# A chunked state space layer on three engines: inputs spread between two turns, three banks for the state products, a row broadcast moved behind the loop

## The reference

```python
def s5_mixer(x, lam_re, lam_im, log_dt, b_re, b_im, c_re, c_im, d_skip, w_glu, w_out):
    u = x.astype(f32).reshape(bsz, seq, N_GROUPS_2, SSM_GROUP)     # 64 groups of 16 channels
    ...
    bu_re = jnp.einsum('bsgc,gpc->bsgp', u, bb_re)                 # 64 complex states a group
    bu_im = jnp.einsum('bsgc,gpc->bsgp', u, bb_im)
    ...
    _, _, h_re, h_im = lax.associative_scan(_complex_linear_combine, (a_re_t, a_im_t, bu_re, bu_im), axis=1)
    y = (jnp.einsum('bsgp,gcp->bsgc', h_re, c_re) - jnp.einsum('bsgp,gcp->bsgc', h_im, c_im))
    y = y + d_skip.reshape(N_GROUPS_2, SSM_GROUP) * u
    y = jax.nn.gelu(y.reshape(bsz, seq, D_MODEL)).astype(x.dtype)
    val, gate = jnp.split(y @ w_glu, 2, axis=-1)
    return (val * jax.nn.sigmoid(gate)) @ w_out
```

## Time and profile before

| | before |
|---|---|
| median of three runs | 1990.58 us (1989.95 to 1991.3) |
| profiled execution | 1992.84 us |
| its span, first to last instruction | 1991.1 us |
| mean granted TensorE clock | 0.906 |
| TensorE busy | 1655.8 us (83%) |
| VectorE busy | 539.9 us (27%) |
| ScalarE busy | 211.1 us (11%) |
| GpSimd busy | 76.0 us (4%) |
| DMA queues, mean | 271 GB/s |

### The profile page before, as it was taken

One profiled execution on the slowest core, in us unless ns is written; L12 is line 12 of the kernel. 1 busy time (PEld: TensorE's weight loads), 2 busy tenths in 40 slices (PEclk: granted clock), 3 DMA queues, 4 the chain that ended last, 5 costly groups with the idle time before them and its releaser, 6 DMA issues. The chain is left out here.

```text
span 1991.1 us, 29124 instructions
## 1 busy us (share of the span) xinstructions
PE 1655.8 (83%) x13147; PEld 1114.5 (56%) x13147; DVE 539.9 (27%) x1285; ACT 211.1 (11%) x484; POOL 76.0 (4%) x96
## 2 busy tenths in 40 slices
PE   7999768889976999856546556689999999999998
PEld 5655435567544885534324333577786446578743
DVE  5752233432333314214211011630210022421002
ACT  2311011000100001100100000110110003211000
POOL 2000000000000100000000000320000000000000
PEclk9989889887998999978778787899999999799999
DMA  9356999998899745999999999534434334134410
GB/s 335 135 204 274 379 422 420 419 421 354 339 421 373 272 197 239 382 420 418 419 416 415 413 414 391 222 128 169 159 137 169 115 118 173 39 133 164 154 57 21
DMA packets 104442, 540.11 MB, mean 271 GB/s; under 512 B 7326, under 2 KB 9438, under 8 KB 86908
## 3 DMA queue, kind: packets, MB, share of 16 engines
q1 hardware_dynamic: 102428, 531.24, 67.0%
q0 software_dynamic: 1888, 6.95, 1.0%
HBM read 531.89 MB, written 6.29 MB: 270 GB/s over the span
## 5 line engine op out<-in xcount | busy, mean ns | idle before, releaser
L712 PE MATMUL ps<-ring,work 128*32 128x256 f32 x3968 | 285.3, 451 | 223.6 <-DMA ring<-in_moe_w_up 223.1
L712 PEld LDWEIGHTS ps<-ring,work 128*32 128x32 f32 x3968 | 158.5, 129 | 342.3 <-issue 295.6
L663 PE MATMUL ps<-hT,ring 128*128 128x256 f32 (+2 forms) x1488 | 329.5, 384 | 2.6 <-DMA ring<-in_lru_w_in 2.6
L689 PE MATMUL ps<-ring,work 128*128 128x512 f32 x768 | 331.0, 592 | 0.0
L663 PEld LDWEIGHTS ps<-hT,ring 128*128 128x128 f32 x1488 | 282.9, 191 | 47.9 <-issue 5.9
L689 PEld LDWEIGHTS ps<-ring,work 128*128 128x128 f32 x768 | 145.7, 190 | 182.2 <-issue 181.3
L724 PE MATMUL ps<-ring,multi 128*32 128x256 f32 x1984 | 127.1, 399 | 16.5 <-ACT multi L1391 12.1
L1956 DVE TENSOR_TENSOR rowb<-rowb,ps 128x128 f32<-128x128 f32 x64 | 18.4, 287 | 354.0 <-ACT rowb L1386 354.0
L1962 DVE COPY multi<-ps 128x256 f32<-128x256 f32 x64 | 27.2, 425 | 283.3 <-PE ps L724 283.3
L732 PE MATMUL ps<-rowb,hres 128*128 128x128 f32 (+1 forms) x640 | 101.9, 299 | 0.2 <-DVE rowb L1622 0.2
L724 PEld LDWEIGHTS ps<-ring,multi 128*32 128x32 f32 x1984 | 60.6, 114 | 62.9 <-ACT multi L1391 18.5
(11 more groups left out here) (434 smaller groups left out, 1363.2 us busy)
## 6 DMA issues: line engine op xcount, KB each, us to landing
ring<-in_moe_w_gate SPq DMA_DIRECT2D x62, 2048.0 KB, 18.8
ring<-in_moe_w_up SPq DMA_DIRECT2D x62, 2048.0 KB, 23.4
ring<-in_moe_w_down SPq DMA_DIRECT2D x62, 2048.0 KB, 21.1
ring<-in_w_ff SPq DMA_DIRECT2D x32, 2048.0 KB, 7.8
ring<-in_sc_w_in SPq DMA_DIRECT2D x6, 2048.0 KB, 17.9
ring<-in_lru_w_in SPq DMA_DIRECT2D x4, 2048.0 KB, 18.4
ring<-in_ssm_w_glu SPq DMA_DIRECT2D x4, 2048.0 KB, 18.7
ring<-in_lru_w_out SPq DMA_DIRECT2D x2, 2048.0 KB, 20.8
```

The costliest lines, as they stand in the source:

```text
L663: mm = pe.matmul(ps[:, bank, 0:n], w[:, k, P * c:P * c + P], hT[:, k, t0:t0 + n], start=(k == 0), stop=(k == DC - 1))
L689: mm = pe.matmul(ps[0:m, 2 + 2 * b + hf, :], left[:, kk, t0:t0 + m], w[:, k, 512 * hf:512 * hf + 512], start=(kk == 0), stop=(kk == 4 * la ...
L712: mm = pe.matmul(ps[32 * q:32 * q + 32, bank, 0:256].rearrange("p (u n) -> p u n", u=2), x[:, k, :], gu[:, k, :, P * q:P * q + P], start=( ...
```

## The change

- TensorE turns block one, waits for the statistics of the second block's norm (`ffn1_var`, 2), spreads block one, and only then turns and spreads block two. The scalar engine copies the spread inputs of block one between the turns' copies of the two blocks.
- The state products go round three banks (0, 1, 7) in place of two, wait for the rotation three groups back, and are issued a group earlier, ahead of the far product.
- Behind the near product of turn 1 TensorE issues six matmuls of `keep_busy`.
- The second half is brought back into banks 5 and 6, too, behind the first Gelu. Of the first pair of the gated projection, four of eight k-steps of both value and gate are issued behind the first Gelu alone.
- On GpSimd the broadcast of the rows of "s5" moves from ahead of the loop to behind it, and in its old place stands an addition of two columns (`pool_pair`) that nobody reads.

```diff
@@ -54,6 +54,7 @@
 SC_BANKS = ((4, 5, 2), (3, 6, 7))
 CONV_A, CONV_B = 4, 3
 SG, SC, SS = 64, 16, 64
+STATE_BANKS = (0, 1, 7)
 ST = SG * SS // P
 HEADS, NOPE, ROPE, VH = 8, 128, 64, 128
 QL, KVL = 384, 256
@@ -158,6 +159,7 @@
         marks = sb("marks", [P, MAX_ROUNDS - 1])
         first_rows = sb("first_rows", [P, 1])
         even_odd = sb("even_odd", [P, 2])
+        pool_pair = sb("pool_pair", [P, 2])
         eps_t = sb("eps_t", [P, 3])
         stats = sb("stats", [P, 3, 12])
         mean_var = sb("mean_var", [P, 3, 4])
@@ -602,7 +604,7 @@
                 pool.dma_start(tab_dram[t, :, 0:n], work[:, at_:at_ + n]).then_inc(S("tabs_stored"), 16)
             pool.wait_ge(*nth("down1", EXTRA + 1))
             broadcast_rows("ffn1")
-            broadcast_rows("s5")
+            nc.gpsimd.tensor_tensor(pool_pair[:, :], ones[:, 0:2], ones[:, 0:2], ALU.add)
             def s5_by_sine(g):
 
                 b = g % 2
@@ -623,6 +625,7 @@
                     nc.gpsimd.tensor_tensor(v[:, 1], p1[:, 1], p2[:, 0], ALU.subtract).then_inc(S("s5_v"), 1)
                 if g >= 1:
                     s5_by_sine(g - 1)
+            broadcast_rows("s5")
             broadcast_rows("mlp0")
             broadcast_rows("mla")
 
@@ -1039,7 +1042,6 @@
             rows_out("mix1", [1, 2], ["sc_out0", "sc_out1"], sc_z, NMETA, "sc_z")
             moe(1)
 
-            transposes("ffn1", [1, 2], "ffn1_normed", bank=6)
             b_map = ring[:, place["s5_tab1"], :].rearrange("p (s i n) -> p s i n", s=ST, i=2)
             w_map = ring[:, place["s5_tab2"], :].rearrange("p (s i n) -> p s i n", s=ST, i=2)
             t_map = ring[:, place["s5_tab0"], 0:2048].rearrange("p (s n) -> p s n", s=ST)
@@ -1059,13 +1061,13 @@
 
             def s5_in(g):
 
-                if g >= 2:
-                    pe.wait_ge(*nth("s5_rotated", g - 1))
+                if g >= 3:
+                    pe.wait_ge(*nth("s5_rotated", g - 2))
                 for t in range(4):
                     s = 4 * g + t
                     for i in range(2):
                         for r in halves:
-                            mm = pe.matmul(ps[r, g % 2, P * t + 64 * i:P * t + 64 * i + 64], b_map[r, s, i, :], s5_u[r, s, :],
+                            mm = pe.matmul(ps[r, STATE_BANKS[g % 3], P * t + 64 * i:P * t + 64 * i + 64], b_map[r, s, i, :], s5_u[r, s, :],
                                            start=True, stop=True)
                 mm.then_inc(S("s5_bu"), 1)
 
@@ -1095,7 +1097,9 @@
             def s5_back(h):
 
                 pe.wait_ge(*nth("s5_y", 4 * h + 4))
-                bank = (5, 0)[h]
+                if h == 1:
+                    pe.wait_ge(*nth("s5_g", 1))
+                bank = 5
                 lines = s5_yr.rearrange("p (m q) c -> p m q c", q=4)
                 for k in range(CHUNK):
                     for q in range(4):
@@ -1104,34 +1108,41 @@
                 mm.then_inc(S("s5_back"), 1)
 
             pe.wait_ge(*nth("sel_ready", 1))
-            s5_inputs(0)
-            s5_inputs(1)
+            for i in range(2):
+                transposes("ffn1", [1, 2], "ffn1_normed", only=i, bank=6)
+                if i == 0:
+                    pe.wait_ge(*nth("ffn1_var", 2))
+                s5_inputs(i)
             pe.wait_ge(*nth("s5_u_act", 2))
             pe.wait_ge(*nth("s5_u_dve", 2))
             for name in ("s5_tab0", "s5_tab1", "s5_tab2"):
                 slot_wait(pe, name)
+            s5_in(0)
             for g in range(DC + 2):
-                if g < DC:
-                    s5_in(g)
+                if g + 1 < DC:
+                    s5_in(g + 1)
                 if g >= 2:
                     s5_far(g - 2)
                 if g < DC:
                     s5_near(g)
+                if g == 1:
+                    keep_busy(6)
                 if g == 6:
                     s5_back(0)
             s5_back(1)
-            pe.wait_ge(*nth("s5_g", 2))
             for m in range(DC):
-                for i, kind in enumerate("vg"):
-                    name = f"glu_{kind}{m // 4}"
-                    if m % 4 == 0:
-                        slot_wait(pe, name)
-                    if m >= 2:
-                        pe.wait_ge(*nth("glu_done", m - 1))
-                    w = slot_view(name, DC, 512)
-                    for k in range(DC):
-                        mm = pe.matmul(ps[:, 2 * (m % 2) + i, 0:SEQ], w[:, k, P * (m % 4):P * (m % 4) + P], s5_g[:, k, :],
-                                       start=(k == 0), stop=(k == DC - 1))
+                if m >= 2:
+                    pe.wait_ge(*nth("glu_done", m - 1))
+                for k0, k1 in (((0, 4), (4, DC)) if m == 0 else ((0, DC),)):
+                    pe.wait_ge(*nth("s5_g", 1 if k1 == 4 else 2))
+                    for i, kind in enumerate("vg"):
+                        name = f"glu_{kind}{m // 4}"
+                        if m % 4 == 0:
+                            slot_wait(pe, name)
+                        w = slot_view(name, DC, 512)
+                        for k in range(k0, k1):
+                            mm = pe.matmul(ps[:, 2 * (m % 2) + i, 0:SEQ], w[:, k, P * (m % 4):P * (m % 4) + P], s5_g[:, k, :],
+                                           start=(k == 0), stop=(k == DC - 1))
                 mm.then_inc(S("glu_proj"), 1)
             rows_out("s5", [1, 2], ["s5_out0", "s5_out1"], s5_y, NMETA, "glu_done")
 
@@ -1359,6 +1370,13 @@
                     A(s5_sines[:, 0], s5_sines[:, 1], ACT.Sin, scale=2 * PI_IN).then_inc(S("rot_ready"), 1)
                     act.wait_ge(*nth("rot_ready", 2))
                     A(s5_sines[:, 1], s5_sines[:, 1], ACT.Sin, scale=-2 * PI_IN).then_inc(S("rot_ready"), 1)
+
+            def s5_inputs_out(i):
+
+                u_of = s5_u.rearrange("p (m q) c -> p q m c", q=4)
+                act.wait_ge(*nth("s5_spread", i + 1))
+                A(u_of[:, 0:2, :, 32 * i:32 * i + 32], ps[:, 4 * i:4 * i + 2, 0:SEQ].rearrange("p q (m c) -> p q m c", m=DC), ACT.Copy)\
+                    .then_inc(S("s5_u_act"), 1)
 
             def moe(l):
                 blocks = moe_blocks[l]
@@ -1423,7 +1441,11 @@
                     A(meta_acc[:, 2, :], ps[:, 5, 0:NMETA], ACT.Sqrt, scale=1.0 / D, bias=eps_t[:, 0:1]).then_inc(S("meta_sd"), 1)
                 evac_turned(f"ffn{l}", blocks[-2:], bank=6, only=0)
                 deviations(f"ffn{l}", only=1)
+                if l == 1:
+                    s5_inputs_out(0)
                 evac_turned(f"ffn{l}", blocks[-2:], bank=6, only=1)
+                if l == 1:
+                    s5_inputs_out(1)
 
             evac_turned("x", [0, 1, 2])
 
@@ -1468,11 +1490,6 @@
                 A(sc_cg[m % 2], ps[:, SC_BANKS[m % 2][0], 0:TC], ACT.Copy).then_inc(S("sc_cg_out"), 1)
             moe(1)
 
-            u_of = s5_u.rearrange("p (m q) c -> p q m c", q=4)
-            for i in range(2):
-                act.wait_ge(*nth("s5_spread", i + 1))
-                A(u_of[:, 0:2, :, 32 * i:32 * i + 32], ps[:, 4 * i:4 * i + 2, 0:SEQ].rearrange("p q (m c) -> p q m c", m=DC), ACT.Copy)\
-                    .then_inc(S("s5_u_act"), 1)
             for g in range(DC + 1):
                 if g < DC:
                     act.wait_ge(*nth("s5_summed", g + 1))
@@ -1481,7 +1498,7 @@
                     h = g // 8
                     act.wait_ge(*nth("s5_back", h + 1))
                     A(s5_g[:, 4 * h:4 * h + 4, :].rearrange("p m (c k) -> p k m c", k=CHUNK),
-                      ps[:, (5, 0)[h]:(5, 0)[h] + 2, :].rearrange("p b (k m c) -> p (b k) m c", k=2, m=4), ACT.Gelu_apprx_tanh)\
+                      ps[:, 5:7, :].rearrange("p b (k m c) -> p (b k) m c", k=2, m=4), ACT.Gelu_apprx_tanh)\
                         .then_inc(S("s5_g"), 1)
             for m in range(DC):
                 act.wait_ge(*nth("glu_proj", m + 1))
@@ -2148,7 +2165,7 @@
                 dve.wait_ge(*nth("s5_bu", g + 1))
                 if g >= 2:
                     dve.wait_ge(*nth("s5_v", g - 1))
-                bu = ps[:, b, :].rearrange("p (t i c) -> p i t c", t=4, i=2)
+                bu = ps[:, STATE_BANKS[g % 3], :].rearrange("p (t i c) -> p i t c", t=4, i=2)
 
                 def by(t):
                     return t[:, 4 * g:4 * g + 4, :].unsqueeze(1).to_broadcast([P, 2, 4, NCH])
```

## The result

| | before | changed |
|---|---|---|
| median of seven runs | 1990.58 us | 1976.32 us |
| lowest | 1985.58 us | 1966.4 us |
| ratio, 95% interval | | 0.9926 [0.9905, 0.9946] |
| profiled execution | 1992.84 us | 1980.01 us |
| its span | 1991.1 us | 1978.3 us |

Foretold were 1975.4 us, 1973.3 to 1980.6, and 0.97 for faster. One run of the first set, at 2504.6 us with a mean clock of 0.631, is left out of the ratio but stands in the median of seven; without it the median is 1973.65 us.

A forecast was written before the change was run, and what follows sets the result against it. VectorE was taken to bound the layer's three-engine ring. Gains of 1.65 + 3.05 + 5.9 + 0.6 + 4.0 = 15.2 us turn the median 1990.58 into 1975.4 us (chance 0.58), range 1973.3 to 1980.6.

The forecast's parts named there:

- What bounds the layer: State space layer's loop: VectorE is the slowest of three engines, 3.95 us a group against TensorE's 3.48; 4.0 taken.
- Rotation 2 to 7: Loop, third to last rotation: three banks and earlier state products cut 25.92 us to 20.0, gain 5.9 us (5.2 to 6.2).
- GpSimd's gap: Before the loop's first addition: a program change after the row broadcast, avoided by the new order; gain 3.05 us (2.8 to 3.5).
- The end: Behind rotation 7: 0.6 us (0 to 1.2) to the last far product, then 4.0 us (2.1 if the clock dips).
- The inputs: Ahead of the first state product: spreading block one before turning block two gains 1.65 us (1.3 to 1.8).
- It starts at 1257.6: Inputs: spreading of block one starts then, after the first block's copies (1257.56) and second block's statistics (1256.80), instead of 1260.92.
- Rival (b): Clock dips once, in the ring or at the projection, costing 1.9 or about 2 us: 1977.3 us; chance 0.15.
- Rival (a): GpSimd's gap comes from a first addition or long idling, so the early pair buys nothing: 1978.5 us; chance 0.10.
- (c): Loop: VectorE and GpSimd slow each other to 4.6 us a group, 3 us less gain: 1978.4 us; chance 0.12.
- (d): TensorE stays at half clock through the whole ring, 7.0 us a group, 12.7 us slower: 2003.3 us; chance 0.02.
- The six matmuls: Before the first far product: 2.9 us and no cost at full clock, 5.8 us at half; no gain counted alone.
- The run-to-run spread: Whole kernel: 0.7 us of spread between runs, allowed at the low side of the range.

The follow-up runs named there:

- second set: The changed kernel, unaltered, measured once more in six runs: median 1968.11 us, ratio to the kernel before 0.9907 [0.9874, 0.9939].

## Why the prediction was right, and where it was not

The forecast held, and of the five terms of its sum four held in size; the inputs came out with the wrong sign.

**What bounds the layer**: right. VectorE sets the pace at 3.94 us a group once the products come early, 3.95 was read from the earlier trace rows.

**Rotation 2 to 7** (5.9 us foretold, 6.24 measured): right, for the reason given, the order of issue. I had named the two edits of the ring together; the runs give all to one.

**GpSimd's gap** (3.05 foretold, 3.63 measured): the place and the price were right, the moment wrong. I put the change of program at the first instruction of the other kind and so had the pair added early. From a broadcast to an addition it is paid from the end of the broadcast on, and moving the rows is the whole gain: 7.25 us before, 7.16 with the rows ahead again. The pair itself stood 9.14 to 10.85 us behind its broadcast in the eleven profiles that have it, where the DMA engines are 0.99 busy with expert weights; whether that is why isn't shown. The 5.87 us of the earlier trace rows I read wholly as this change, but they hold a DMA that landed 2.0 us behind its issue at 1412.45, so 4.4 us are left. The Trainium skill (GPSIMD Engine Reference, Instruction dispatch) puts about 6 us, invisible in the profile, at the first call into fresh code. The idle times behind a broadcast fit that in kind and are 1 to 5 us longer. With the rows ahead the 7.16 us are paid although an addition had run before, at 844.62, so not at a first call alone.

**The end** (0.6 and 4.0 foretold, 0.47 and 3.83 measured): right, and the clock's part of it as well: without the split all 3.8 us came back. The 0.6 is there where the clock stays at 1.00 behind rotation 7 (10.34 to 10.36), and not in the run with three banks only (10.81, clock 0.66 from 1310 to 1315).

**The inputs** (1.65 us won foretold, 1.93 lost measured): wrong. The failed step is "It starts at 1257.6". I took the end of the first turn's copies (1257.56) from the earlier trace rows as it stood, and did not ask what had set it. It was the ten idle matmuls, whose end at 1256.01 was harmless as long as the second block's norm (1259.64) came later. The new order made the first turn matter and so put them on the path. They also started later: 3.45 us behind the anchor, with 3.17 to 3.45 in every profile but that of before (2.54), and took 7.47 for 6.81 us at a lower clock. The late start is no work of the change, since the kernel before with only the rows moved has 3.34. Then the clock fell twice more: the second turn took 1.97 us instead of 1.29 and it was 2.08 us instead of 1.26 from the first state product's start to rotation 0. Of 3.6 us missed, 1.7 are the later start of spreading (0.9 for the late start of the idle matmuls, 0.7 for their length), 1.1 the longer course from there to the product, 0.8 the product itself. Why before's own profile has the early 2.54, I can't say.

**Rival (b)**, a dip of the clock, did not come where it was placed: the six added matmuls took 3.18 us, near the 2.9 of a full clock, and the projection ran at 1.00. But two dips came ahead of them, in the inputs and at the first state products, where I had reckoned with none because the pauses were under 0.9 us. They were, and the clock fell nonetheless. **Rival (a)** is out by the run without the pair, though the pair bought nothing all the same, for another reason. **(c)** is out by 3.94 us a group. **(d)** did not come; nearest to it is the run with the rows moved alone, whose clock is between 0.50 and 0.93 in every 5 us from 1275 to 1320.

**The six matmuls**: "at the full clock they cost nothing", right; they also bring nothing to a ring that has the new order.

**The run-to-run spread** was the step that I sized worst. I allowed 0.7 us from three runs; the six runs behind the changed kernel's ratio span 15 us, and its second set 14. The lower end of the range is a slip too: the upper ends and 0.7 us give 1973.2, not 1973.3. The upper end fits (a) with (b), about 1980.5, but (a) with (c) would give 1981.5.

## What to carry to other kernels

When three engines pass work round a ring, issue the next input of the slowest engine ahead of whatever waits for the ring's output; an extra buffer without that order won 0.6 us here, the order without the buffer 4.6. When a stall is taken away, ask whether the engine behind it can keep up at its worst clock: one edit alone gave back all of its 3.5 us. And before a step is moved up, look at what set the start of its input, even where that once cost nothing. What looks like a gain or a loss of a few microseconds in one run of this kernel may be the clock of a stage that no edit touches.

## What the runs showed of the hardware that I had not expected

Attention, whose code is the same in every kernel here, took 115.29 to 127.12 us. In the fourteen profiles it goes with the granted clock over two stretches. Six have a clock of 1.00 throughout in windows of 5 us and took 115.29 to 115.54 us. Three have one short dip, 25 to 35 us behind the stage's start, and took 116.95 to 117.24. The five above 121 have a clock of 0.50 for 10 us or more some 60 us behind the start. Three windows over that second stretch, of the kernel before, of the changed kernel and of the one without the early addition:

```profile
1696.00:1716.00 20.00, 20.00 (x64) 13.45 (x62) 10.07 (x39) 6.11 (x24) 0.00 (x0) 0.50 0.08 29
```

```profile
1687.00:1707.00 20.00, 19.86 (x74) 13.05 (x72) 10.86 (x43) 6.11 (x24) 0.00 (x0) 0.62 0.08 31
```

```profile
1675.00:1705.00 30.00, 27.91 (x143) 18.66 (x143) 17.83 (x71) 14.39 (x48) 0.00 (x0) 1.00 0.38 137
```

In the kernel before, the clock stood at 0.50, which is 1.2 GHz, for all of these 20 us, and the profile shows no pause of TensorE in them; since it models the ends of matmuls, short ones could hide. The Trainium skill (TensorE: Matmul & The Clock Gate, Part 1) says that activity releases the half rate; that stretch, of small matmuls in a chain with VectorE and ScalarE, does not agree. What starts the dip in one run and not in another, no run here shows. Luck of this kind is worth 12 us, as much as the whole change, and decides single runs of this kernel.
